# Sliding-window attention inside a fused two-block kernel: who rotates the queries, and when the weight loads and the second rotation are issued

## The reference

```
q = rope(x @ w_q) * 128 ** -0.5      # 3 groups x 8 heads x 128
k = rope(x @ w_k); v = x @ w_v       # 3 groups x 2 kv heads; a kv head serves 4 q heads
for (window, dilation) in ((128, 1), (512, 4), (2048, 16)):
    o_g, lse_g = banded attention of q_g over k_g, v_g with that dilation
o = sum_g softmax_g(lse_g) * o_g     # the three groups are mixed by their log-sums
y = (o * silu(x @ w_z)) @ w_out
rope(x) = [x1 * cos - x2 * sin, x2 * cos + x1 * sin]   # x1, x2: the halves of the 128 features
```

## Time and profile before

| | |
|---|---|
| median of 3 runs | 3221.51 us (3218.53 to 3221.86) |
| the profiled execution's own time | 3223.74 us |
| its span in the profile | 3221.9 us |
| PE (TensorE matmul) | 2815.3 us busy, 87% |
| PEld (TensorE weight load) | 2312.6 us, 72% |
| DVE (VectorE) | 1603.6 us, 50% |
| ACT (ScalarE) | 1122.0 us, 35% |
| POOL (GpSimd) | 1042.0 us, 32% |
| mean granted TensorE clock | 0.948 |

### The profile page before, as it was taken

How to read it: one execution, slowest core, us unless ns; L and a number is a source line. 1 busy time by engine, 2 the same in 40 slices (tenths; PEclk the granted TensorE clock), 3 DMA queues, 4 the chain that set the end, 5 groups by cost and what they waited for, 6 DMA issues and landing times. The chain is left out here.

```text
span 3221.9 us, 39379 instructions
## 1 busy us (share of the span) xinstructions
PE 2815.3 (87%) x14688; PEld 2312.6 (72%) x14688; DVE 1603.6 (50%) x1750; ACT 1122.0 (35%) x1789; POOL 1042.0 (32%) x520
## 2 busy tenths in 40 slices
PE   6998988689999999968299999999787979999887
PEld 5776776578788888756177877777575757878775
DVE  5553455813666156648736556556442133444344
ACT  3122122223333133431425555555412234433331
POOL 3452451255555564403043333333021330000001
PEclk8999998899999999989599999999898989999998
DMA  3010104332111221134111111111121110000011
GB/s 118 27 32 20 32 26 162 127 109 67 52 53 47 57 63 46 46 130 145 61 53 40 40 40 33 34 40 40 59 73 51 39 39 14 7 13 7 12 67 65
DMA packets 52939, 176.06 MB, mean 55 GB/s; under 512 B 8800, under 2 KB 10464, under 8 KB 52832
## 3 DMA queue, kind: packets, MB, share of 16 engines
q1 hardware_dynamic: 45920, 149.38, 15.0%
q10 hardware_dynamic: 6912, 25.17, 2.2%
HBM read 133.46 MB, written 16.94 MB: 47 GB/s over the span
## 5 line engine op out<-in xcount | busy, mean ns | idle before, releaser
L108 POOL TENSOR_SCALAR w_hi<-w_raw 128x1024 fp32r<-128x1024 f32 x156 | 180.4, 1156 | 1995.1 <-PE pj L134 693.5
L132 PE MATMUL pj<-x_hi,w_hi 128*128 128x512 f32 x1132 | 454.1, 401 | 63.4 <-PEq L580 24.6
L133 PE MATMUL pj<-x_lo,w_hi 128*128 128x512 f32 x1132 | 446.4, 394 | 0.0
L134 PE MATMUL pj<-x_hi,w_lo 128*128 128x512 f32 x1132 | 445.7, 394 | 0.0
L110 POOL TENSOR_TENSOR w_lo<-w_raw,w_hi 128x1024 fp32r<-128x1024 f32 x156 | 390.6, 2504 | 23.3 <-issue 8.1
L1058 PE MATMUL pj<-x_hi,w_hi 128*128 128x512 f32 x704 | 292.8, 416 | 34.4 <-PEq L580 34.4
L132 PEld LDWEIGHTS pj<-x_hi,w_hi 128*128 128x128 f32 x1132 | 216.4, 191 | 114.0 <-issue 65.4
L1060 PE MATMUL pj<-x_hi,w_lo 128*128 128x512 f32 x704 | 275.7, 392 | 0.0
L1059 PE MATMUL pj<-x_lo,w_hi 128*128 128x512 f32 x704 | 275.4, 391 | 0.0
L1479 PE MATMUL pj<-x_hi,w_hi 128*128 128x512 f32 x512 | 223.9, 437 | 35.6 <-DVEq L1686 26.2
L134 PEld LDWEIGHTS pj<-x_hi,w_lo 128*128 128x128 f32 x1132 | 216.0, 191 | 46.2
(11 more groups left out here) (330 smaller groups left out, 5506.0 us busy)
## 6 DMA issues: line engine op xcount, KB each, us to landing
w_raw<-w_slots SPq DMA_DIRECT2D x158, 512.0 KB, 3.6
out_ada_rows<-ada_t ACTq DMA_DIRECT2D x48, 512.0 KB, 5.0
swa_swapped<-swa_q SPq DMA_DIRECT2D x60, 256.0 KB, 3.7
x_res<-o_t SPq DMA_DIRECT2D x12, 1024.0 KB, 4.0
o_t<-x_res SPq DMA_DIRECT2D x12, 1024.0 KB, 7.1
o_t<-x_t SPq DMA_DIRECT2D x8, 1024.0 KB, 10.9
da_swapped<-da_raw SPq DMA_DIRECT2D x64, 128.0 KB, 2.3
out_t<-o_t SPq DMA_DIRECT2D x4, 1024.0 KB, 4.4
```

What stands on the lines that cost most here:

```text
L108: nc.gpsimd.tensor_scalar(g.w_hi[:, u, :], g.w_raw[:, u, :], 1.0, 0.0, ALU.mult, ALU.add)
L132: nc.tensor.matmul(dst, w_hi, x_hi[:, k, cols], start=(j == 0), stop=False)
L133: nc.tensor.matmul(dst, w_hi, x_lo[:, k, cols], start=False, stop=False)
L134: mm = nc.tensor.matmul(dst, w_lo, x_hi[:, k, cols], start=False, stop=(j == n - 1))
```

## The change

- **Rotation.** VectorE multiplies a projected half by cosine straight out of PSUM into `swa_q` (`cosine`, `turn_q`). After it ScalarE copies the two 64-partition halves, swapped, out of PSUM into `swa_swapped` (`evacuate`, two copies). The DMAs of the swap and GpSimd's cosine product are gone; GpSimd waits for ScalarE (`j_act`). The next slot's half is written only when both are done.
- **Pieces.** Up to two follow each step of the scores (16 in all); 16 to 19 stand ahead of the transposition of the log-sums, 20 to 27 between the two, 28 and 29 after the second, 30 and 31 behind the first two steps of pass two.
- **GpSimd.** The first split and rotation of the next slots no longer wait for the totals; the second split does; the second rotation waits until all ten steps of pass two are scaled.
- **SyncE.** The loads: two at the head's start, two after the totals are back; in the last head its one load comes after the totals.
- **ScalarE and VectorE.** The gates, swaps and cosine products are put to other places, as the diff shows.

```diff
-        GAP, FIRST_T, COVER, FILL = 10, 13, 25, 27
+        WITH_SCORES = (0, 2, 4, 6, 8, 10, 11, 12, 14, 15, 16)
+        FIRST_T, COVER, FILL = 20, 28, 30
...
         @block.sync
             def head(kv, hh, h, nxt):
-                load(z, 1)
+                if nxt:
+                    load(z, 1)
+                    load(z + 1, 0)
                 sp.wait_ge(m.lt_ready, h + 1)
...
-                if nxt:
-                    swap(qs, 0, nz, rope, False, False)
                 sp.wait_ge(m.total_ready, h + 1)
...
-                if nxt:
-                    load(z + 1, 0)
                 sp.wait_ge(m.total_out, h * 48 + 48)
...
                 if nxt:
-                    for j in (1, 2):
-                        swap(qs, j, nz + j, rope + j, False, False)
-                        load(z + (1 + j), (1 + j + 1) % 2)
+                    load(z + 2, 1)
+                    load(z + 3, 0)
+                else:
+                    load(z, 1)
...
         @block.gpsimd
-            def rope(kind, j, index, count):
-                pool.wait_ge(swapped[j % 2], count * 32 + 32)
+            def rope(kind, j, nz):
+                pool.wait_ge(m.j_act, nz * 2 + 2)
                 nc.gpsimd.tensor_tensor(swp[:, j % 2, :], swp[:, j % 2, :], sin[:, :], ALU.mult)
-                nc.gpsimd.tensor_tensor(qs[:, j, :], qs[:, j, :], cos[:, :], ALU.mult)
...
                     for j in range(G):
-                        if j == 0:
+                        if j == 1:
                             pool.wait_ge(m.total_ready, h + 1)
                         split_slot(nc, pool, g, s0 + z + 3 + j, hh * 4)
+                        if j == 1:
+                            pool.wait_ge(m.p_ready, h * N + N)
+                        rope(nxt, j, nz + j)
...
         @block.scalar
             def evacuate(kind, b, slot, half, turned):
...
+                    act.wait_ge(m.j_dve, turned * 2 + half + 1)
+                    E2 = SWA_E // 2
+                    nc.scalar.copy(swp[0:E2, b, cols[half]], g.pj[E2:SWA_E, 0, cols[half]])
+                    c = nc.scalar.copy(swp[E2:SWA_E, b, cols[half]], g.pj[0:E2, 0, cols[half]])
...
                 for i in range(N):
                     exp(i)
-                    if nxt and i in (4, 8):
-                        gate(i // 8)
+                    if nxt and i in (2, 4):
+                        gate(i // 4)
+                    if i == 7:
+                        take(0, 0)
                 act.drain()
                 nc.scalar.activation(spread(lse[:, :]), dense(den[:, :]), ACT.Ln).then_inc(m.ln_ready, 1)
-                take(0, 0)
+                take(0, 1)
+                act.wait_ge(m.lt_done, h + 1)
+                nc.scalar.copy(lse_t[:, :], turn(0)[0:96, 0:P]).then_inc(m.lt_ready, 1)
                 if not nxt:
                     gate(0)
-                act.wait_ge(m.lt_done, h + 1)
-                nc.scalar.copy(lse_t[:, :], turn(0)[0:96, 0:P]).then_inc(m.lt_ready, 1)
-                take(0, 1)
+                take(1, 0)
...
-                take(1, 0)
                 take(1, 1)
+                take(2, 0)
...
                 for i in range(N):
-                    if FILL + i == 28:
-                        take(2, 0)
-                    if FILL + i == 32:
+                    take_p(i)
+                    if i == 2:
                         take(2, 1)
-                    take_p(i)
...
         @block.vector
+            def cosine(j, slot, half):
+                if half == 0:
+                    dve.wait_ge(m.half_done, slot + 1)
+                else:
+                    dve.wait_ge(g.slot_done, slot + (s0 + 1))
+                nc.vector.tensor_tensor(qs[:, j, cols[half]], proj(half), cos[:, cols[half]], ALU.mult).then_inc(m.j_dve, 1)
...
                 for i in range(N):
                     shift(i)
-                    if nxt and i in (5, 9):
-                        gate(i // 9)
+                    if nxt and i in (3, 5):
+                        gate(i // 5)
+                    if i == 7:
+                        turn_q(0, 0)
...
+                turn_q(0, 1)
+                turn_q(1, 0)
...
+                turn_q(1, 1)
+                turn_q(2, 0)
...
                 for i in range(N):
                     normalize(i)
+                    if i == 4:
+                        turn_q(2, 1)
```

More of the change, by code:

```diff
@@ L932, in rope_index, with dve_slots @@
             return kv * ROPES + (j if kind == "k" else G + j)
-        def swap_count(kind, j, kv):
-            return kv * 10 + (2 if kind == "q" else 0) + j // 2 if j % 2 == 0 else kv * 5 + (1 if kind == "q" else 0)
+        def dve_slots(kind, slot, kv):
+            return slot - G * (kv if kind == "k" else kv + 1)
         def sequence(engine, alone, head):
@@ L1047, in _, with piece @@
         def _(pe):
-            def piece(slot, u, e, free):
+            def piece(slot, u, e, *free):
                 half, q = divmod(e, 4)
@@ L1053, in piece @@
                         pe.wait_ge(g.w_ready, slot + (s0 + 1))
-                    if free is not None:
-                        pe.wait_ge(free[0], free[1] + half)
+                    for done, value in free:
+                        pe.wait_ge(done, value + half)
                 for k in (2 * q, 2 * q + 1):
@@ L1075, in alone @@
                 pending = None
+                before = "k"
                 for kind, j, slot, nz in standalone(kv):
+                    free = []
+                    if slot > 0:
+                        free.append((m.j_act, nz * 2 - 1))
+                        if before != "v":
+                            free.append((m.j_dve, dve_slots("k" if kind == "v" else kind, slot, kv) * 2 - 1))
+                    before = kind
                     for e in range(8):
-                        piece(slot, slot % 2, e, (m.j_act, nz * 2 - 1) if nz else None)
+                        piece(slot, slot % 2, e, *free)
                         if pending and e == 2:
@@ L1090, in fill @@
                     for e in range(lo, hi):
[L1091 to L1095, removed]
+                        j = e // 8 - 1
+                        free = [(m.j_dve, (z + (1 + j - G * (kv + 1))) * 2 - 1)]
+                        if j != 0:
+                            free.append((m.j_act, (nz + max(j, 0)) * 2 - 1))
+                        if j < 0 or nxt:
+                            piece(z + (1 + j), j % 2, e % 8, *free)
                 def scores(i):
@@ L1142, in head @@
                     if nxt:
-                        fill(i, i + 1)
-                fill(*((GAP, FIRST_T) if nxt else (0, 4)))
+                        fill(WITH_SCORES[i], WITH_SCORES[i + 1])
+                fill(*((WITH_SCORES[N], FIRST_T) if nxt else (0, 4)))
                 pe.wait_ge(m.lse_ready, h + 1)
@@ L1154, in head @@
                         turn_p(i)
-                    if nxt:
+                    if nxt and FILL + i < 32:
                         fill(FILL + i, FILL + i + 1)
@@ L1164, in _, with evacuate @@
             act.sem_inc(m.pt_evac, 2)
-            def evacuate(dst, slot, nz, half):
+            def evacuate(kind, b, slot, half, turned):
                 if half == 0:
@@ L1171, in evacuate @@
                     act.wait_ge(g.slot_done, slot + (s0 + 1))
-                nc.scalar.copy(dst, proj(half)).then_inc(m.j_act, 1)
+                if kind == "v":
+                    c = nc.scalar.copy(swp[:, b, cols[half]], proj(half))
+                else:
[3 more added lines that the diff above has]
+                    c = nc.scalar.copy(swp[E2:SWA_E, b, cols[half]], g.pj[0:E2, 0, cols[half]])
+                c.then_inc(m.j_act, 1)
             def take_values(kv, j):
@@ L1182, in alone @@
                     for half in range(2):
[L1183 to L1191, removed]
+                        if half == 0 and kind == "v" and j < 2:
+                            act.wait_ge(m.rope_ready, kv * ROPES + (2 + j))
+                        elif half == 0 and kind == "q" and j < 2:
+                            act.wait_ge(m.vt_done, kv * G + (2 + j))
+                        elif half == 0 and kind != "v" and j == 2:
+                            act.wait_ge(m.rope_ready, rope_index(kind, j, kv) - 1)
+                        evacuate(kind, (j + 1) % 2 if kind == "v" else j % 2, slot, half, dve_slots(kind, slot, kv))
                         if pending is not None and half == 0:
@@ L1276, in _, with turn_q @@
             dve.drain()
-            def alone(kv):
-                pass
-            def head(kv, hh, h, nxt):
+            def cosine(j, slot, half):
+                if half == 0:
+                    dve.wait_ge(m.half_done, slot + 1)
+                else:
+                    dve.wait_ge(g.slot_done, slot + (s0 + 1))
+                nc.vector.tensor_tensor(qs[:, j, cols[half]], proj(half), cos[:, cols[half]], ALU.mult).then_inc(m.j_dve, 1)
+            def alone(kv):
+                for kind, j, slot, nz in standalone(kv):
```

(12 more changed lines are left out.)

27 lines of the change are left out of this document (4 added, 23 removed).

## The result

The changed kernel takes 3192.8 us (3192.6 to 3194.5, 4 runs), the kernel before beside it 3220.5 (3218.5 to 3221.9, 4 runs): a ratio of 0.9915, 95% interval [0.9902, 0.9929]. It is 27.7 us faster where I forecast 8, and 1.2 us under my range. In the profiles the attention stage ends 27.7 us earlier (1391.42 for 1419.12). What follows it, where the kernels are alike, is 3.2 us shorter too; the profiled execution of before took 3223.7 us, 3.3 above its median, so I don't count this to the change.

The account below looks back on a forecast made before the run. TensorE was taken as the bound, some 4.5 us per head to win. Terms -8.6 - 28 - 4.3 + 21.4 + 1.7 + 9.6 = -8.2 us gave 3215.5 from 3223.7, 3213.5 as median; range 3194 to 3226.

Parts of the forecast that it names:

- Last head: Last head's hops: load behind hops and copy ahead of gate -11.4, collisions +2.3 and late rotations +0.5; -8.6 us.
- Pass two: Pass two of seven heads: scalings freed of GpSimd's rotation, so waits of 4.0 us per head go; -28 us.
- pass two stays late: Rival: ScalarE's swap and `turn_q(2, 1)` take the place of pass two's waits, 1.0 us a head; 3220.5, chance 0.15.
- The k head's surplus: Head feeding the next k: its 4.3 us over a repeating head, from strided rotations and half clock, go; -4.3 us.
- Where TensorE's cover goes: Between the log-sums' and totals' transpositions: pieces fall from 12 to 8, waits grow 3.05 us per head, +21.4 for seven.
- the last maximum: End of the scores: the last 128x4 maximum stands behind GpSimd's first split operation, +0.97 us.
- rotation 0 misses the additions: Rival, log-sum hop: additions escape GpSimd's rotation 0, wait falls to 1.5 us, clock cost stays; 3193, chance 0.13.
- The k head's +1.7: Head feeding the next k: strided rotation 0 is some 1.7 us longer beside the hop's first addition; +1.7 us.
- The clock: After the new 2.95 us wait at the totals' transposition: half speed costs 1.37 us per head, +9.6 for seven.
- the four fifths: Share taken of the 1.7 us lost per half-speed stretch, over heads that do and don't fall: 1.37 us.
- the held rotations' sum: Rotation 1, a split and rotation 2 after the last scaling end 24.3 us after the totals' transposition; they don't bite.
- Thin cover decides: Rival, between the two transpositions: two half-clock stretches per head and longer hops make it slower; 3229, chance 0.12.

Follow-up runs that it names:

- The best kernel: Kernel before with the hold, SyncE's loads out of both hops, and the last head's log-sum copy ahead of the gate; old rotation kept: 3171.8 us, ratio 0.9849.
- The added piece: Changed kernel with piece 28 ahead of the totals' transposition, nine pieces of cover instead of eight: 3180.3 us, ratio 0.9873.

## Why the forecast had the direction right and the size wrong

**Last head:** forecast -8.6, measured -8.1 (from its first scores to its last weighted sum 63.6 us before, 55.5 now). The expected collision with the split is there: the two additions take 2.4 us more than their 0.28 each, where I had 2.3.

**Pass two:** forecast -28, measured -30.8. From T to the head's end it was 27.79 us with seven pieces and is 19.31 with four: 27.79 - 3 x 1.36 - 19.31 = 4.4 per head. The weight loader's 4.5 us in the earlier trace rows was the better row than PE's 3.3, and my 4.0 between them was short. That GpSimd's work beside the scalings was the reason is shown twice: the hold alone brings it to the kernel before, its removal takes it from the kernel after. The rival "pass two stays late" falls.

**The k head's surplus:** forecast -4.3, measured so: 79.1 is now 72.3 us (977.09 to 1049.42), as the others.

**Where TensorE's cover goes is the first step that failed, by size.** Forecast +3.05 us per head and +1.7 in the k head; measured 14.13 + 4 x 1.36 - 17.86 = +1.7 per head, +12.0 for seven, and nothing more in the k head. The mechanism held: the wait at the totals grew from 1.2 to 2.4, and a piece given back to the cover takes 1.9 of it away. Of the 1.3 us that I put too high, 1.0 is the last maximum. I let it arrive 0.07 us behind the split and lose 0.97; it arrived 0.01 us ahead. The copy of the log-sums began 0.40 us after their transposition (0.34 before), where I had 1.44 behind the swap, and piece 20 waited 0.25 us, not 1.3. With the maximum made to come second, the 1.0 came back. Rotation 0 did catch the first addition (L1342), for 0.74 us (1.13 for 0.39) where I had 1.4, because the hop before took 3.84 us and not 3.33, with a load ahead of it in SyncE's queue; from the copy of the log-sums to T it came out nearly as forecast (13.5 for 13.6 us). The rival that rotation 0 misses the additions names nearly the measured time, 3193, but not what happened; the nearness is chance, and by its own sum it was 3194. The k head's +1.7 was an error of reading: the first group of k has stride 1, and its rotation 0 takes 2.39 us like the others.

**The clock is the second.** Forecast 1.37 us per head on average, 9.6 in all; measured two heads of seven at 1.6, 3.2. The price of one fall was right, the four fifths were not. They came from a single wait of 2.63 us, and the waits here are 2.4. Both profiles of the changed kernel had two in seven; others with waits of that length had two, three and six.

Sum: -8.1 - 30.8 - 4.3 + 12.0 + 3.2 = -28.0, measured -27.7. The two costs were 17.5 us too high together, and pass two 2.8 too low. (3215.5 less 2.2 is 3213.3 and not the 3213.5 that I wrote, and the held rotations' sum comes to T + 24.0, not 24.3; neither matters.)

**Which part brings what.** The hold brings 31 us, alone or in the change. The last head's load brings 5.5 alone and 9 in the change. The rest of the change, taken together, costs: the cosine product and swap from PSUM, the pieces moved, rotation 0 and its split ahead of the totals, and the loads at the head's start. The best kernel has none of it and is 21 us faster, 2.6 us in each of seven heads and 3.2 of clock, less 1 in the last head. The rearranged order has TensorE run out of pieces at the totals, which the old one doesn't, once SyncE's load is out of the hop. The added piece gives about half of that back (12.5 us), rotation 0 behind the totals 6.6, and both together no more than the piece. What each of the other parts costs wasn't measured by itself. Whether the new rotation with the old twelve pieces of cover would reach the best kernel stays open; it wasn't run. "Thin cover decides" was wrong as a forecast, but names what holds the change back.

**The port.** The rule that I cited from the Trainium skill (page SBUF — State Buffer, section "SBUF: two separate sides"), an exclusive lock for a whole instruction to whoever starts first, agrees with the rows here: the same maximum takes 0.17 us where it starts 0.01 us ahead of the split and 0.81 us where it starts 0.28 behind it, and there are 8x128 operations with two inputs, of 1.13, 0.85 and 2.45 us, that end within 0.3 us after GpSimd's.

## What to carry to other kernels

Where short VectorE operations feed the bound engine, look for GpSimd work that shares their port and can start later: one wait on GpSimd was worth as much here as the whole rearrangement, and that its work came later cost nothing. Count the cover at each round trip before moving pieces from it; a transfer queued ahead of a round trip is cheaper to move than to cover. Where two operations start within 0.1 us of each other, price both orders and keep both in the range: the order was worth 1 us per head at the last maximum, and 1.5 us of waiting went with it at the first scaling.

## What the runs showed of the hardware

- The clock after a wait of TensorE isn't told by its length alone. At the totals it fell behind none of seven waits of 1.5 to 2.0 us, behind 2, 2, 2, 3 and 6 of seven of 2.4 to 2.6 us (in five profiles), and behind all seven of 4.4 to 4.9. In the kernel without the hold it also fell behind a pass-two wait of 1.54 us in two of six heads, the two in which it had fallen at the totals. In one kernel a wait of 2.38 us was followed by 0.58 of the clock and one of 2.51 by 1.00. A fall behind a wait at the totals costs 1.6 us.
- An 8x128 VectorE operation with two inputs, 0.37 to 0.39 us, takes up to 2.45 beside a GpSimd operation: size is no protection.
- A ScalarE copy from PSUM of 64x512 takes 0.58 us (row at 943.45 above), as one of 128x512 does; swapping two halves of the partitions costs two full copies.
